# Long convolution inside a fused layer: transform of u by even and odd times, spectrum products and gates laid out anew

## The reference, cut to what matters

```
z_hy, q, k, v, gates = split(h @ w_in)
x0, x1, v = split(short_conv(z_hy))
u = v * x1
uf, kf = rfft(u, n=512), rfft(kernel, n=512)      # along time, 256 tokens
y = irfft(uf * kf)[:256] + u * hy_bias            # long convolution
y_hy = (y * x0) @ w_hy_out
o = rmsnorm(softmax(q k) v - lam * softmax(q' k') v') # differential attention, 8 heads
g_hy, g_da = sigmoid(gates)
out = (g_hy * y_hy + g_da * (o @ w_da_out)) @ w_o
```

## Time and profile before

| | |
|---|---|
| median of 3 runs | 1270.52 us (1270.29 to 1270.6) |
| the profiled execution | 1268.89 us |
| its span (first to last instruction) | 1267.1 us |
| granted TensorE clock, mean | 0.997 of full speed |
| weave, by the trace | about 835 to 1018 us |

### The profile page before, as it was taken

How to read it: one execution, slowest core, us unless ns; L and a number is a source line. 1 busy time by engine, 2 the same in 40 slices (tenths; PEclk the granted TensorE clock), 3 DMA queues, 4 the chain that set the end, 5 groups by cost and what they waited for, 6 DMA issues and landing times.

```text
span 1267.1 us, 19254 instructions
## 1 busy us (share of the span) xinstructions
PE 1236.4 (98%) x7645; PEld 1090.2 (86%) x7645; DVE 883.0 (70%) x1439; ACT 585.7 (46%) x927; POOL 100.5 (8%) x103
## 2 busy tenths in 40 slices
PE   6999999999999999999999999999999998999997
PEld 6987999978888888887787998888789997999986
DVE  5986889797787777753424776367886676777744
ACT  7656545555622222222325752246345645544533
POOL 2130001000000000001100012001420000000000
PEclk9999999999999999999999999999999999999999
DMA  7634777777366668853332543333233554655562
GB/s 290 208 137 150 230 240 242 235 237 240 106 220 199 194 245 296 282 195 103 114 133 75 164 153 100 97 113 116 89 104 100 199 167 139 191 179 181 181 195 84
DMA packets 59753, 219.28 MB, mean 173 GB/s; under 512 B 6844, under 2 KB 7136, under 8 KB 58896
## 3 DMA queue, kind: packets, MB, share of 16 engines
q1 hardware_dynamic: 56736, 205.42, 49.8%
q0 software_dynamic: 2352, 11.76, 2.7%
q10 hardware_dynamic: 576, 0.88, 0.2%
HBM read 216.95 MB, written 1.07 MB: 172 GB/s over the span
## 4 chain that ended last, share of the span: by engine, by line
PE 85%; DVE 6%; ACT 5%; issue 2%; DMA 1%; POOL 0%; DVEq 0%; ACTq 0%
PE ps L2179 19%; PE ps L2180 18%; PE ps L2181 18%; PE ps L2227 4%; PE ps L2228 4%; PE ps L2229 4%; PE ps L2238 3%; PE ps L2240 3%; PE ps L2239 3%; ACT hi L711 2%; PE ps L2216 1%; PE ps L2215 1%; PE ps L2217 1%; PE ps L2760 1%; DVE lo L1344 1%
## 5 line engine op out<-in xcount | busy, mean ns | idle before, releaser
L1344 DVE TENSOR_TENSOR lo<-raw,hi 128x1024 fp32r<-128x1024 f32 x315 | 388.4, 1234 | 249.8 <-ACT hi L711 246.8
L2179 PE MATMUL ps<-nh,hi 128*128 128x256 f32 (+2 forms) x1776 | 552.1, 311 | 4.3 <-DVE lo L1344 1.3
L711 ACT ACTIVATE hi<-raw 128x1024 fp32r<-128x1024 f32 x315 | 333.0, 1058 | 474.4 <-PE ps L2181 273.5
L2181 PE MATMUL ps<-nl,hi 128*128 128x256 f32 (+2 forms) x1776 | 544.4, 307 | 0.0
L2180 PE MATMUL ps<-nh,lo 128*128 128x256 f32 (+2 forms) x1776 | 544.3, 306 | 0.0
L2179 PEld LDWEIGHTS ps<-nh,hi 128*128 128x128 f32 x1776 | 338.6, 191 | 35.2 <-issue 15.7
L2180 PEld LDWEIGHTS ps<-nh,lo 128*128 128x128 f32 x1776 | 338.7, 191 | 16.3 <-issue 1.2
L2181 PEld LDWEIGHTS ps<-nl,hi 128*128 128x128 f32 x1776 | 338.5, 191 | 15.3
L1331 DVE SCALAR_TENSOR_TENSOR raw<-raw,cvec 128x1024 f32<-128x1024 f32 x72 | 86.8, 1222 | 1.4
L2227 PE MATMUL ps<-hi,H 128*128 128x512 f32 x176 | 69.1, 393 | 1.1 <-DVE lo L1344 1.1
L2238 PE MATMUL ps<-hi,H 128*128 128x512 f32 x176 | 69.4, 394 | 0.2 <-DVE ygx L1823 0.2
(11 more groups left out here) (384 smaller groups left out, 1381.9 us busy)
## 6 DMA issues: line engine op xcount, KB each, us to landing
raw<-in_up SPq DMA_DIRECT2D x132, 512.0 KB, 3.7
raw<-in_in SPq DMA_DIRECT2D x86, 512.0 KB, 3.5
raw<-in_w_ada SPq DMA_DIRECT2D x72, 512.0 KB, 4.6
raw<-in_down SPq DMA_DIRECT2D x66, 512.0 KB, 3.6
raw<-in_out SPq DMA_DIRECT2D x8, 512.0 KB, 3.6
raw<-in_hy_out SPq DMA_DIRECT2D x8, 512.0 KB, 3.4
raw<-in_da_out SPq DMA_DIRECT2D x8, 512.0 KB, 3.9
raw<-in_o SPq DMA_DIRECT2D x8, 512.0 KB, 3.5
```

Source lines behind the costliest of these rows:

```text
L711: act.activation(hi[:, h, 0:n], raw[:, r, 0:n], ACT.Copy).then_inc(hi_done, 1)
L1344: dve.tensor_tensor(lo[:, h, 0:w], raw[:, r, 0:w], hi[:, h, 0:w].bitcast(F32), ALU.subtract).then_inc(lo_done, 1)
L2179: mm(o, hi[:, h, wk], x_hi, start=first, stop=False)
L2181: return mm(o, hi[:, h, wk], x_lo, start=False, stop=last)
```

## The change

The transform of u uses the even and odd times: with E the product over even times and O the one over odd times, at frequencies of the lower half, E + O is the lower half of the spectrum and E - O the upper half. So a step makes two products instead of four; the four `spectrum(g)` are now (half of the features, cosine or sine). What moves with it:

- `turn_u` transposes every second column of u (`tt:T:2`), and `ut` holds even and odd times.
- A step leaves E in bank 2 and O in bank 3. ScalarE copies O to a new tile `uodd`; VectorE adds and subtracts (both read bank 2 and `uodd`) into `yt`, then multiplies the two results by `kre` and `kim`, four products whose inputs are all in SBUF. Cosine products go straight to `spec_im` and `proj`, sine products stay in `kim` and `kre`.
- GpSimd starts only in the second step of each half of the features: four sums and differences in place and the four folds, as many as before.
- The third and fourth step are at p = 15 and 17, the inverses at p = 18 to 21 and 23 to 26.
- A gate lies where its own half of the features had its spectrum (tiles over both `kre` and `kim`), so `gate_hy` waits for four parts and `gate_da` for eight. A sigmoid's tile is a strided view of the same size.
- The square sums of `otok` go from VectorE to ScalarE, behind `take_out`.
- The DFT constant has 8 tiles instead of 16: the forward ones were a set of their own, and now those of the kernel's spectrum serve.

```diff
-SPECTRUM_AT = (10, 12, 14, 16)
-GATE_AT = (0, 1, 4, 5, 2, 3, 6, 7)
+SPECTRUM_AT = (10, 12, 15, 17)
+INVERSE_AT = (18, 19, 20, 21, 23, 24, 25, 26)
+GATE_AT = (0, 1, 4, 5, 8, 9, 12, 13, 2, 3, 6, 7, 10, 11, 14, 15)
...
-        dft = place(92 * KB, "dft_s", [P, 16, P])
+        dft = place(92 * KB, "dft_s", [P, 8, P])
+        uodd = place(96 * KB, "uodd", [P, 2, 512])
@@ GpSimd
-                pool.wait_ge(sem("re_products"), g + 1)
-                pool.tensor_tensor(halves(proj, ft, half), yt[:, 0:2, :], yt[:, 2:4, :], ALU.subtract)
-                pool.wait_ge(sem("im_products"), g + 1)
-                pool.tensor_tensor(halves(spec_im, ft, half), ki, kr, ALU.add).then_inc(sem("yf_ready"), 1)
+                for ft in range(2):
+                    re, im = halves(proj, ft, half), halves(spec_im, ft, half)
+                    pool.wait_ge(sem("u_products"), 8 * half + 2 * ft + 6)
+                    pool.tensor_tensor(re, re, ki, ALU.subtract).then_inc(sem("yf_ready"), 1)
+                    pool.tensor_tensor(im, im, kr, ALU.add).then_inc(sem("yf_ready"), 1)
+                pool.wait_ge(sem("yf_ready"), 4 * half + 4)
...
@@ ScalarE
+                act.wait_ge(sem("otok_ready"), r + 1)
+                act.activation(rtmp[:, 0:P], otok[:, r, :], ACT.Square,
+                               accum_out=small[:, 192 + r:193 + r]).then_inc(sem("oss_ready"), 1)
...
-                        act.wait_ge(sem("yf_ready"), x.j // 2 + 1)
+                        act.wait_ge(sem("yf_ready"), 4 if name == "gate_hy" else 8)
+                    if p in SPECTRUM_AT:
+                        g = SPECTRUM_AT.index(p)
+                        act.wait_ge(sem("uf_ready"), g + 1)
+                        if g >= 2:
+                            act.wait_ge(sem("u_folded"), g - 1)
+                        act.activation(uodd[:, g % 2, :], ps[:, 3, :], ACT.Copy).then_inc(sem("uodd_copied"), 1)
@@ VectorE
-                step(dve.tensor_tensor(t0, kr, ur, ALU.mult))
-                dve.tensor_tensor(t1, ki, ui, ALU.mult).then_inc(sem("re_products"), 1)
-                step(dve.tensor_tensor(ki, ki, ur, ALU.mult))
-                dve.tensor_tensor(kr, kr, ui, ALU.mult).then_inc(sem("im_products"), 1)
+                dve.wait_ge(sem("uodd_copied"), g + 1)
+                step(dve.tensor_tensor(flat(low), ps[:, 2, :], uodd[:, g % 2, :], ALU.add))
+                dve.tensor_tensor(flat(high), ps[:, 2, :], uodd[:, g % 2, :], ALU.subtract)\
+                   .then_inc(sem("u_folded"), 1)
+                dve.wait_ge(sem("u_folded"), g + 1)
+                for ft, part in enumerate((low, high)):
+                    to = (halves(spec_im, ft, half), halves(proj, ft, half)) if kind == 0 else (ki, kr)
+                    for k, y in zip((ki, kr), to):
+                        dve.tensor_tensor(y, k, part, ALU.mult).then_inc(sem("u_products"), 1)
...
-                    if 3 <= p <= 33 and p % 2:
-                        square_sum((p - 3) // 2)
@@ TensorE
-                                     u[:, 4 * half + j, tt * P:tt * P + P], ident)
+                                     u[:, 4 * half + j, tt:T:2], ident)
...
-                    pe.wait_ge(sem("im_products"), g)
-                for kind in range(2):
-                    for tt in range(2):
-                        o = mm(ps[:, 2 + kind, :], dft[:, 4 * kind + 2 * tt + ft, :], ut_half(tt, half),
-                               start=(tt == 0), stop=(tt == 1))
+                    pe.wait_ge(sem("u_folded"), g)
+                for odd in range(2):
+                    o = mm(ps[:, 2 + odd, :], dft[:, 2 * kind + odd, :], ut_half(odd, half), start=True, stop=True)
...
-                    pe.wait_ge(sem("im_products"), 4)
+                    pe.wait_ge(sem("u_folded"), 4)
```

More of the change, by code:

```diff
@@ L85, in constants @@
     by_parity = np.concatenate([t[::2], t[1::2]])
[L86 to L90, removed]
+    dft = np.zeros((P, 8, P), np.float32)
     for m, w in enumerate((np.cos(th), np.sin(th))):
         halves = w[by_parity, :P].reshape(2, P, P)
-        dft[:, 8 + 2 * m:10 + 2 * m] = halves.transpose(1, 0, 2)
-        dft[:, 12 + m:16:2] = halves.transpose(2, 0, 1) / 256
+        dft[:, 2 * m:2 * m + 2] = halves.transpose(1, 0, 2)
+        dft[:, 4 + m:8:2] = halves.transpose(2, 0, 1) / 256
     bands = 16
@@ L665, in _ @@
                     .then_inc(sem("u_ready"), 1)
-            for g in range(4):
-                half, ft = g // 2, g % 2
+            for half in range(2):
                 w = slice(half * 512, half * 512 + 512)
-                kr, ki = (k[:, ft, w].rearrange("p (a n) -> p a n", a=2) for k in (kre, kim))
-                pool.wait_ge(sem("re_products"), g + 1)
-                pool.tensor_tensor(halves(proj, ft, half), yt[:, 0:2, :], yt[:, 2:4, :], ALU.subtract)\
-                    .then_inc(sem("re_summed"), 1)
-                pool.wait_ge(sem("im_products"), g + 1)
-                pool.tensor_tensor(halves(spec_im, ft, half), ki, kr, ALU.add).then_inc(sem("yf_ready"), 1)
[L675 to L683, removed]
+                for ft in range(2):
+                    kr, ki = (k[:, ft, w].rearrange("p (a n) -> p a n", a=2) for k in (kre, kim))
+                    re, im = halves(proj, ft, half), halves(spec_im, ft, half)
[3 more added lines that the diff above has]
+                pool.wait_ge(sem("yf_ready"), 4 * half + 4)
+                for m, y in enumerate((proj, spec_im)):
+                    low, high = halves(y, 0, half), halves(y, 1, half)
+                    pool.tensor_tensor(ut_half(m, half), low, high, ALU.add).then_inc(sem("folded"), 1)
+                    pool.wait_ge(sem("folded"), 4 * half + 2 * m + 1)
+                    pool.tensor_tensor(high, low, high, ALU.subtract).then_inc(sem("folded"), 1)
             pool.wait_ge(sem("o2_ready"), 2 * HEADS2)
@@ L1977, in mix_maps @@
                    .then_inc(sem("pmix_ready"), 1)
[L1979 to L1985, removed]
             def largest(r):
@@ L1994, in spectrum, with flat @@
             def spectrum(g):
-                half, ft = g // 2, g % 2
-                pair = "p (a n) -> p a n"
+                half, kind = g // 2, g % 2
                 w = slice(half * 512, half * 512 + 512)
[L1998 to L2004, removed]
+                low, high = (yt[:, 2 * n:2 * n + 2, :] for n in range(2))
+                def flat(a):
+                    return a.rearrange("p a n -> p (a n)")
+                dve.wait_ge(sem("uodd_copied"), g + 1)
+                if g == 0:
                     dve.wait_ge(sem("kernel_folded"), 4)
-                step(dve.tensor_tensor(t0, kr, ur, ALU.mult))
-                dve.tensor_tensor(t1, ki, ui, ALU.mult).then_inc(sem("re_products"), 1)
+                step(dve.tensor_tensor(flat(low), ps[:, 2, :], uodd[:, g % 2, :], ALU.add))
+                dve.tensor_tensor(flat(high), ps[:, 2, :], uodd[:, g % 2, :], ALU.subtract)\
+                   .then_inc(sem("u_folded"), 1)
                 after(n)
-                dve.wait_ge(sem("re_products"), g + 1)
-                step(dve.tensor_tensor(ki, ki, ur, ALU.mult))
-                dve.tensor_tensor(kr, kr, ui, ALU.mult).then_inc(sem("im_products"), 1)
+                dve.wait_ge(sem("u_folded"), g + 1)
+                for ft, part in enumerate((low, high)):
+                    kr, ki = (k[:, ft, w].rearrange("p (a n) -> p a n", a=2) for k in (kre, kim))
+                    to = (halves(spec_im, ft, half), halves(proj, ft, half)) if kind == 0 else (ki, kr)
+                    for k, y in zip((ki, kr), to):
+                        dve.tensor_tensor(y, k, part, ALU.mult).then_inc(sem("u_products"), 1)
             def convolved(j):
@@ L2803, in _ @@
                         spectrum(SPECTRUM_AT.index(p))
-                    if 18 <= p < 26:
-                        inverse(p - 18)
+                    if p in INVERSE_AT:
+                        inverse(INVERSE_AT.index(p))
                     if p >= 36:
```

22 lines of the change are left out of this document (11 added, 11 removed).

## The result

Slower: 1274.95 us, median of 6 runs (1274.3 to 1278.6), against 1270.69 for the kernel before (6 runs): ratio 1.0041, 95% interval 1.003 to 1.0051. The profiled execution took 1274.89 us, its span 1273.1, its mean clock 0.994. The time was above the predicted range, which ended at 1274.2, and on the side of the second rival, though not by its mechanism.

What follows compares the result with a forecast made beforehand. TensorE, busy 98% of the span, was taken as the bound. Profiled: -6.88 steps, +8.0 or +5.5 waits, +0.5 scaling, middle +0.3, so 1269.2; plus 1.63 gives 1270.8 us, range 1264.6 to 1274.2.

Steps and rivals of the forecast that it cites:

- the second rival: Mix loses more turns: the factor of `mix_maps` also takes turns with GpSimd, waiting 11.5 us, 1274.6 us; chance 0.15.
- TensorE, right: Spectrum steps on TensorE: two products instead of four, four blocks of 1.72 us, 6.88 us removed.
- Turns, right: VectorE operations with both inputs in SBUF alternate with GpSimd's, a whole operation each; a turn costs about 1.25 us.
- the list of signs: Expected trace: a few products of 1.9, GpSimd sums 1.9 to 2.4, mix waits 6 to 9 us at positions 15 to 21.
- the heads' scaling: Root for the scaling of all heads, behind ScalarE's last square: TensorE waits there, +0.5 us.
- The middle of +1.6 and -0.9: Total change of profiled execution, taken midway between two cases of GpSimd turns in the weave: +0.3 us, 1269.2.
- the first end: GpSimd wins every turn in the weave: 9.0 us of TensorE waiting, +8.0 against now, total +1.6.
- the other end: GpSimd never gets between two products in the weave: 6.5 us of TensorE waiting, +5.5 against now, total -0.9.
- the 1.63 that was added for the median: Whole kernel: median of the runs taken to lie 1.63 us above the profiled execution, 1270.8 against 1269.2.
- The queue sum: Engine queues laid side by side in the weave: TensorE waits 2.8, 2.1, 0.8, 2.3 us at positions 15, 17, 19, 21.
- the first rival: Saving comes through: turns in the weave matter little, 1.7 us of waiting without them, 1264.8 us; chance 0.27.
- the third rival: Strided transposes in `turn_u` cost TensorE time, +2.0 us on the forecast, 1272.8 us; chance 0.04.

Runs made afterwards that it cites:

- e1: Changed kernel with GpSimd's sixteen spectrum sums, differences and folds cut to one column of every 256, the rest left out: 1267.41 us, ratio 0.998 to before.
- e10: e7 with the products' inputs back in SBUF, as in the change: 1271.26 us, ratio 1.0015 to the kernel before.
- e7: Changed kernel with products reading PSUM, late slabs' taps ahead of the spectrum step, fourth step and inverses later; all computed: 1264.85 us, ratio 0.9964 to before.
- e3: Changed kernel plus eight needless TensorE products where it waits, before slabs 15 and 17 and position 21's transposes: 1272.02 us, ratio 1.0019 to before.
- e4: Changed kernel with only the sixteen square sums moved back from ScalarE to VectorE: 1276.47 us, ratio 1.0053 to before.
- e8: Control: kernel before, with only late slabs' taps moved ahead of the spectrum step or inverse in VectorE's queue: 1269.94 us, ratio 1.0006.
- e2: Changed kernel with sum and difference written back to PSUM for the products, banks released later, first four inverses one position later: 1270.13 us, ratio 1.0003 to before.
- e9: e7 with the taps put back behind the spectrum step: 1269.16 us, ratio 0.9994 to the kernel before.
- e5: Changed kernel with only late slabs' taps moved ahead of the spectrum step or inverse in VectorE's queue: 1272.88 us, ratio 1.0022 to before.

## Why the prediction was wrong

**TensorE, right.** Sixteen pieces, four blocks of 1.72.

**Turns, right.** They are the largest part of what makes this change lose: 7.5 us by e1, 6.4 by e10 against e7, both with the clock that hangs on them. The product of 1.78 and the remainder of 2.30 are as the list of signs had them, and sums of up to 2.24. The mix (1.21 instead of 0.75) pays about the rest of a turn that the working gave it, the 128x2 scaling (1.20) a turn that it hadn't. (The Trainium skill, SBUF — State Buffer, Who interferes with whom, says that with at most one SBUF input, outside its two-port modes, VectorE doesn't contend. That is e7's edit, and its products of 0.68 beside GpSimd agree.)

**The clock, missing: the step that failed.** No step has a price for what TensorE does behind a wait; the prediction put it at nothing without a reason. Its waits sum to 9.0, with the heads' scaling 9.5; measured are 10.1, and those at positions 15, 17, 19 and 21 make 8.6, inside the "6 to 9 us together" of its signs. So the waiting was about right, and 3.0 us of half-speed work came on top (e3: 2.9). The trace of before had such a drop, though outside the weave, where the earlier trace rows doesn't reach. TensorE waits 1.52 and then 2.34 us there, and the clock behind them is 0.50:

```profile
1068.48 2.54 PE L2304 MATMUL ps<-con,xgr 128*128 128x128 f32 x12 [2.34 <-DVE xgr L2117]
```

```profile
1070.00:1072.00 2.00, 2.00 (x11) 2.00 (x10) 1.54 (x5) 1.79 (x4) 0.00 (x0) 0.50 0.04 8
```

The full clock of the weave in the earlier trace rows therefore said only that a stretch without long waits has a full clock.

**The middle of +1.6 and -0.9, wrong.** The prediction says that the first end "needs GpSimd to win every turn". It won the turn that mattered, between the third and the fourth product: 900.20 for 1.78. The rows of before showed the same pattern, a waiting GpSimd that goes as soon as VectorE's operation ends and a VectorE operation that then takes 1.38. That no row had *products* back to back was no reason for an equal weight to the other end. This is 1.3 us.

So the largest error is a term left out. With the upper end and the clock the same sum gives -6.88 + 8.0 + 0.5 + 3.0 = +4.6, or 1273.5 for a profiled execution that took 1274.89. The rest is 0.7 for longer first pieces, 0.5 of more waiting and 0.2 in front of the stretch. The median looks nearer to the forecast than the working was, by luck: the profiled execution was 5.7 us over its forecast of 1269.2, the median only 4.2 over 1270.8, since the 1.63 that was added for the median turned out as 0.06.

**Position 17, right in size by accident.** The queue sum made TensorE wait for the mix, 2.1 us; it waited 2.36 for its bank. The taps of slab 15 were counted in VectorE's load, but not whom they release. This is why the first rival's "1.7 us of waiting" without turns was wrong too: e1 has 0.81 + 2.36 + 0.88 + 0.66 = 4.7. At position 15 it was also the bank, 4.0 instead of the 2.8 for the mix, and there the mix came after the slab had begun.

**Smaller ones.** Position 19 had 0.4 for 0.8, position 21 1.8 for 2.3, the scaling +0.5 as forecast. The second rival's mechanism fell: at 908.28 the factor takes 0.28 inside GpSimd's operation of 907.97 to 909.26; its time, 1274.6, was near for other reasons. (Its 11.5 us of waiting is also a slip or leaves a step unsaid: 9.0 with the two waits raised from 2.8 to 4.2 and from 0.8 to 2.2 is 11.8.) ScalarE hid squares and copies, as far as the small effect of e4 tells. The strided transposes aren't free. The weight loads of u went from 0.14 us to 0.21, and the chain's two blocks from 1.09 to 1.22 and from 0.87 to 0.96, 0.2 us in all where the third rival had 2.0. By the Trainium skill's stride of four elements (SBUF — State Buffer, on SBUF "cachelines") nothing should change; the loads differ. The two rows are of the kernel before and of the one after (minimum, median, maximum in ns):

```profile
L2749 PEld LDWEIGHTS ps<-con,u x16: 139/140/142, 873.0 to 877.9; 128*128 128x128 f32 x16
```

```profile
L2747 PEld LDWEIGHTS ps<-con,u x16: 194/209/218, 873.0 to 878.1; 128*128 128x128 f32 x16
```

## What to carry to other kernels

Halving TensorE's work in a step exposes the other engines' queues. For each operation there, ask which bank or buffer it releases, not only how long it takes, and put what releases an engine that is 98% busy ahead of long work that nothing waits for soon. Where the steps were still long, in the kernel before, this order was worth nothing (e8).

A product whose second input stayed in PSUM took no turns with GpSimd; here that was worth 6.4 us in the otherwise best layout.

Price a wait of TensorE of some 2 us or more with the half-speed work that may follow, about 1.5 us each time that it did here. Look for such a drop in the whole trace and not only in the stretch that changes, and judge by several executions, since one profile may be the lucky one.

## What the runs showed of the hardware that was not expected

- The granted clock fell to about half (0.50 to 0.54, the level of 1.2 GHz) behind waits of 4.02 and 1.81 us (changed kernel), 2.36 (e1's profile) and 2.48 (e2's profile), and behind 1.52 and 2.34 close after each other in the kernel before. It stayed full behind 2.36 (changed kernel), 2.48 (e9's profile), 2.09 (e7) and 1.78 (e5's profile). So waits of the same length, at the same position, went either way, and the length of the wait alone doesn't decide it. What decides is open.
- Work that nothing uses made a kernel with such waits 2.9 us faster (e3).
- A waiting GpSimd gets in between two products of VectorE that stand back to back without a wait (1.78 instead of 0.68 us).
- VectorE's TENSOR_SCALAR on 128x2 in `largest` takes turns (1.20 us), and the one on 128x1 in `mix_maps` doesn't (0.28 us beside GpSimd at 908.28, and never over 0.276 in sixteen).
